# The last group of the second MLP, taken by token tile across both second-layer granules

## The chip, the cores and the metric

The kernel runs on one core of a Trainium2 chip. The metric is the device time of one execution in microseconds (us). PE is TensorE (matmuls), DVE is VectorE, ACT is ScalarE, POOL is GpSimd, SP is SyncE, which issues most transfers. SBUF is the on-chip memory, PSUM holds the eight banks that matmuls accumulate into.

## What is computed

The reference is a small network on 256 tokens of width 1024. First a block with a convolution and Fourier mixer, cross attention and a mixture of 32 experts, then two layers of attention and MLP. The change concerns only the very last step, the MLP of the second of these layers and the layer norm behind it:

```
def squared_relu_mlp(h, w1, w2):            # w1: 1024 x 4096, w2: 4096 x 1024
    return jnp.square(jax.nn.relu(h @ w1)) @ w2

y = squared_relu_mlp(h, mlp_w1[layer], mlp_w2[layer])
x = layer_norm(DN_ALPHA * x + gate * y, ln_g[layer, 1], ln_b[layer, 1])
```

All inputs are fp32, and the output is the x of 256 x 1024.

## The kernel before

**Precision.** Every fp32 product of this part is made of three matmuls in a rounded type: both operands are split into a rounded part ("hi") and a remainder ("lo"), and `three` (line 1318) issues hi x hi, hi x lo and lo x hi. So a weight granule must be rounded by ACT (`split_hi`, line 561) and its remainder taken by DVE (`split_lo`, line 572) before PE has all of it; the semaphore `w_lo` counts the remainders, and PE waits for it once per granule.

**Tiling.** Weights come in granules of 2 MB into four ring slots. An MLP has 16: even ones are a 512-column slab of `w1`, odd ones the matching 512 rows of `w2`. They are worked off in four groups (`it` = 0 to 3), each of two halves (`p` = 0, 1); half p uses granule 2p of the group for the first layer and granule 2p + 1 for the second. In the last group these are, counted over the MLP, granules 12 to 15.

**First layer of a half.** Two banks (b = 0, 1), each 8 x 2 x 3 = 48 matmuls of 256 columns; the result is the transposed hidden block, two chunks of 128 hidden units for each b. For each b ACT takes the relu (line 1086) and the square of it, rounded (line 1089), into `hid[0]`; DVE squares again in full precision into `sq_h` (line 2787) and subtracts to get the remainder into `hid[1]` (line 2791), counted by `mlp_lo`. In ACT's queue the rounding of the group's granules 2 and 3 (`split_hi`, after half 0) stands behind the square for b = 1, and in DVE's queue the two `split_lo` stand behind the subtraction for b = 1. In half 1 of the last group there is nothing left to split and nothing left to load.

**Second layer of a half.** It accumulates into banks 0 to 3: bank 2t + h is token tile t (128 tokens) and column half h (512 columns). One half of a group takes 2 (b) x 2 (r) x 2 (t) x 2 (h) x 3 = 48 matmuls of 512 columns. Normally the order is b, r, then the four banks. Only in half 1 of the last group it is t, h, b, r, so that the banks are finished one after another; each of the first three increments `ln_y0`, the last one `used`.

**The end.** The layer norm (`layer_norm`, line 2695, DVE) waits for each bank in turn. For each it multiplies with the gate (line 2706), adds the scaled x (line 2707) and takes statistics (line 2708); after both halves of a tile come the aggregate (line 2710), a root on ACT (line 1040), a reciprocal and a product (lines 2713, 2714). Tile 0 is then normalized by ACT (line 1047) and scaled and shifted by POOL (lines 838, 840); tile 1 is finished by DVE itself in two halves (lines 2723, 2724). SP stores tile 0 in one transfer (line 770) and tile 1 in two (line 773). Every engine works its instructions off in the order written; a wait holds up all that stands behind it in that engine's queue.

**Memory.** `hid` lies at 0 to 2047 of the area `arena`, `relu_h` at 2048, `sq_h` at 3072. The words from 4096 to 5119 are not used in the second MLP.

Of the kernel before, what the change touches and what calls it, by code (L numbers as in the profile page):

```python
# [19 lines left out]
F32 = mybir.dt.float32  # L20
# [7 lines left out]
P = 128  # L28
S = 256
TB = S // P  # L30
# [9 lines left out]
HW = 512  # L40
# [198 lines left out]
def build_program(nc, A, tab_d, dft_d, out_d):  # L239
    ctx = ExitStack()  # L240
    with ctx:
# [76 lines left out]
        def arn(a, w):  # L318
            return arena[:, a:a + w]

        def arn_r(a, w):
            return arena_r[:, a:a + w]
# [68 lines left out]
        lng = arn(5264, D)  # L391
        lnb = arn(6288, D)
        hid = [arn_r(a, 1024).rearrange("p (k s) -> p k s", k=4) for a in (0, 1024)]
        relu_h, sq_h = (arn(a, 1024).rearrange("p (k s) -> p k s", k=4) for a in (2048, 3072))

        def late_part(u):
# [447 lines left out]
        def _(act):  # L844
# [230 lines left out]
            def mlp_group(l, it, last, ahead=None, first=False):  # L1075

                n = f"mlp{l}"
                for p in range(2):
                    for b in range(2):
                        c = 2 * p + b + 1  # L1080
                        h = B[b if first and p == 0 else 4 + b]
                        if b == 0:
                            act.wait_ge(*upto(n, "mlp_h", it * 2 + (p + 1)))
                        else:
                            act.wait_ge(used, it * R2 + done(n, 2 * p)[1])
                        act.activation(relu_h[:, 2 * b:2 * b + 2, :], h[:].rearrange("p (k s) -> p k s", k=2),
                                       ACT.Relu, bias=zero).then_inc(sem("mlp_relu"), 1)
                        act.wait_ge(*upto(n, "mlp_relu", it * 4 + c))
                        act.activation(hid[0][:, 2 * b:2 * b + 2, :], relu_h[:, 2 * b:2 * b + 2, :], ACT.Square,
                                       bias=zero).then_inc(sem("mlp_sq"), 1)  # L1090
                    if l == 0 and last and p == 0:
                        act.wait_ge(sem("late_comb"), 12)
                        act.activation(vec[:, 0, :], B[6][:, 0:P], ACT.Copy).then_inc(sem("late_part"), 1)
                    if not (last and p == 1):
                        split_hi(act, n, 2 * p + 2, it)
                        split_hi(act, n, 2 * p + 3, it)
                    if p == 0 and ahead is not None:
                        split_hi(act, *ahead)
                    if l == 0 and last and p == 0:
                        act.wait_ge(sem("late_comb"), 13)  # L1100
                        act.activation(mod[:, 3, :], B[6][:, 256:280], ACT.Copy).then_inc(sem("late_read"), 1)
                    elif l == 0 and last:
                        gate_rows(1)
# [174 lines left out]
        def _(pe):  # L1278
# [676 lines left out]
            def mlp_group(l, it, last, first=False):  # L1955

                n = f"mlp{l}"
                for p in range(2):
                    g = at[0] + 2 * p
                    pe.wait_ge(sem("w_lo"), it * R2 + split_no(g))  # L1960
                    w = chunks(pair(g), KC)
                    if first and p == 0:
                        first_hidden(l, w)
                    for b in range(0 if first and p == 0 else 2):
                        for k in range(KC):
                            if b == 0:
                                x_chunk(2 * l + 1, max(k, 1))
                            for r in range(2):
                                f = 2 * b + r
                                mm = three(B[4 + b][:, r * S:(r + 1) * S], cut3(w, k, f * P, (f + 1) * P),  # L1970
                                           cut3((XT_r, XTL[2 * l + 1]), k, 0, S), k == 0 and r == 0, k == KC - 1)
                        mm.then_inc(sem("mlp_h") if b == 0 else used, 1)
                    if l == 0 and p == 0 and it:
                        unit_sums(it - 1)
                    if l == 0 and p == 1 and last:
                        pe.wait_ge(sem("late_read"), 3)
                        gate_rows(1)
                    g = g + 1
                    halved = l == 0 and first and p == 0
                    if halved:  # L1980
                        pe.wait_ge(sem("lo_part"), 3)
                    else:
                        pe.wait_ge(sem("w_lo"), it * R2 + split_no(g))
                    w = chunks(pair(g), 4)
                    if last and p == 1:
                        for t in range(TB):
                            for h in range(2):
                                for b in range(2):
                                    pe.wait_ge(*upto(n, "mlp_lo", it * 4 + (2 * p + b + 1)))
                                    for r in range(2):  # L1990
                                        mm = three(B[2 * t + h][:], cut3(hid, 2 * b + r, t * P, (t + 1) * P),
                                                   cut3(w, 2 * b + r, h * HW, (h + 1) * HW), False, False)
                                mm.then_inc(sem("ln_y0") if t + h < 2 else used, 1)
                        continue
                    for b in range(2):
                        pe.wait_ge(*upto(n, "mlp_lo", it * 4 + (2 * p + b + 1)))
                        if halved and b:
                            pe.wait_ge(sem("w_lo"), split_no(g))
                        for r in range(2):
                            begin = first and p + b + r == 0  # L2000
                            for t, h in ((0, 0), (1, 0), (1, 1), (0, 1)):
                                if begin and (t, h) == (0, 1):
                                    pe.wait_ge(*upto(n, "mlp_relu", 2))
                                mm = three(B[2 * t + h][:], cut3(hid, 2 * b + r, t * P, (t + 1) * P),
                                           cut3(w, 2 * b + r, h * HW, (h + 1) * HW), begin, False)
                    mm.then_inc(used, 1)
                    if l == 0 and last:
                        pe.wait_ge(sem("late_part"), 13)
                        pe.matmul(B[6][:, 256:280], vec[:, 0, :], ident.rearrange("p (c n) -> p n c", n=32)[:, 0:6, :],
                                  start=True, stop=True).then_inc(sem("late_comb"), 1)  # L2010
# [231 lines left out]
        def _(dve):  # L2242
# [536 lines left out]
            def mlp_group(l, it, last, ahead=None, first=False):  # L2779

                n = f"mlp{l}"
                for p in range(2):
                    for b in range(2):
                        c = 2 * p + b + 1
                        dve.wait_ge(*upto(n, "mlp_relu", it * 4 + c))
                        hb = slice(2 * b, 2 * b + 2)
                        dve.tensor_tensor(sq_h[:, hb, :], relu_h[:, hb, :], relu_h[:, hb, :],
                                          ALU.mult).then_inc(sem("mlp_tt"), 1)
                        dve.wait_ge(*upto(n, "mlp_tt", it * 4 + c))
                        dve.wait_ge(*upto(n, "mlp_sq", it * 4 + c))  # L2790
                        dve.tensor_tensor(hid[1][:, hb, :], sq_h[:, hb, :], hid[0][:, hb, :].bitcast(F32),  # L2791
                                          ALU.subtract).then_inc(sem("mlp_lo"), 1)
                        if first and c == 1:
                            first_out_lo(dve, 1)
                    by_unit = l == 0 and not last
                    if by_unit:
                        unit_rows(2 * it + p, 0, 3)
                    if not (last and p == 1):
                        split_lo(dve, n, 2 * p + 2, it)
                        if by_unit:  # L2800
                            unit_rows(2 * it + p, 3, 5)
                        split_lo(dve, n, 2 * p + 3, it)
                        if by_unit:
                            unit_rows(2 * it + p, 5, 8)
                    if p == 0 and ahead is not None:
                        split_lo(dve, *ahead)
                    if l == 0 and last and p == 0:
                        affine_ready(1)
                        affine("ln0", range(TB))
# [189 lines left out]
```

## Time and profile before

| | us |
|---|---|
| median of 3 runs | 1796.16 |
| lowest of them | 1792.27 |
| highest of them | 1941.92 |
| the profiled execution | 1793.1 |
| its span (first to last instruction) | 1791.3 |

Times in rows are microseconds from the start of the span. A line number is that of the kernel's code; L1321 is the helper `three`, so all split matmuls share it and are told apart by time and by the number of columns. Matmuls overlap: the duration in a row is that of one matmul from start to end, and successive ones start closer together than that.

### The profile page before, as it was taken

The page shows a single profiled execution, that of the slowest core. Times are in us where ns is not written, and L with a number is a line of the kernel's source. Part 1 is how long each engine was busy: PE and PEld are TensorE (multiplying, and loading weights), DVE is VectorE, ACT ScalarE, POOL GpSimd, SP SyncE. Part 2 cuts the span into 40 slices and gives each one's busy share as a digit, 9 for nine tenths or more (in the row PEclk, how much of TensorE's full clock was granted, in tenths as well). Part 3 has the DMA queues.
Part 4 walks back from the last instruction along what each step waited for, and adds up shares of the span by engine and source line. Part 5 has one row for each costly group of instructions (what it writes and reads, how often), then busy time and mean ns, then how long its engine had stood idle before and what let it go on. Part 6 is the DMA issues. An engine that isn't in the chain of part 4 may idle for free.

```text
span 1791.3 us, 24226 instructions
## 1 busy us (share of the span) xinstructions
PE 1724.1 (96%) x9828; PEld 1083.8 (61%) x9828; DVE 777.9 (43%) x1327; ACT 524.1 (29%) x694; POOL 33.8 (2%) x40
## 2 busy tenths in 40 slices
PE   8999999999999999999999999999999999899997
PEld 7878754443443434343434343375799988689986
DVE  4454442221221212121212121289887779676555
ACT  5353421111111111111101010247544455644442
POOL 0002000000000000000000000000000010000001
PEclk9999999999999999999999999998999999999999
DMA  9757999999999999999999999975387754335550
GB/s 347 285 200 289 371 396 429 428 427 427 428 429 428 429 428 428 429 428 429 428 428 429 428 429 428 421 283 201 118 286 269 278 205 177 124 119 188 187 210 24
DMA packets 97287, 587.54 MB, mean 328 GB/s; under 512 B 7822, under 2 KB 8036, under 8 KB 71620
## 3 DMA queue, kind: packets, MB, share of 16 engines
q1 hardware_dynamic: 95744, 582.28, 80.5%
q10 hardware_dynamic: 1476, 4.30, 0.7%
q8 instruction: 50, 0.82, 0.2%
q14 instruction: 17, 0.14, 0.0%
HBM read 585.51 MB, written 1.05 MB: 327 GB/s over the span
## 4 chain that ended last, share of the span: by engine, by line
PE 73%; DMA 20%; DVE 3%; ACT 3%; issue 1%; SPq 0%; DVEq 0%; ACTq 0%
PE bank L1321 32%; DMA ring<-in_w_gate_up 19%; PE bank L1635 15%; PE bank L1654 9%; PE bank L1581 4%; PE bank L1903 3%; PE bank L1665 1%; PE bank L1949 1%; PE bank L1627 1%; PE bank L1406 1%; ACT arena L1003 1%; PE bank L1647 1%; ACT sb_XN L1122 1%; DMA ring<-in_w_k 1%; PE bank L2160 0%
## 5 line engine op out<-in xcount | busy, mean ns | idle before, releaser
L1635 PE MATMUL bank<-ring,arena 128*64 128x512 f32 x2048 | 462.6, 597 | 29.0 <-DMA ring<-in_w_gate_up 28.8
L1635 PEld LDWEIGHTS bank<-ring,arena 128*64 128x64 f32 x2048 | 137.5, 136 | 320.2 <-issue 255.3
L1654 PE MATMUL bank<-ring,arena 128*64 128x512 f32 x1024 | 226.8, 595 | 3.3
L1321 PE MATMUL bank<-w_hi,arena_r 128*128 128x512 f32 x672 | 217.2, 392 | 0.9 <-DVE arena_r L2791 0.9
L572 DVE TENSOR_TENSOR w_lo<-ring,w_hi 128x4096 fp32r<-128x4096 f32 (+2 forms) x43 | 188.0, 4373 | 27.9 <-ACT w_hi L561 26.3
L2498 DVE TENSOR_SCALAR arena<-bank 128x512 f32<-128x512 f32 x32 | 22.1, 692 | 367.6 <-PE bank L1635 367.6
L1001 ACT ACTIVATE arena<-arena,sb_tab 128x512 f32<-128x512 f32 x32 | 23.1, 722 | 508.8 <-DVE arena L2498 508.8
L561 ACT ACTIVATE w_hi<-ring 128x4096 fp32r<-128x4096 f32 (+2 forms) x43 | 152.4, 3586 | 20.4 <-DMA ring<-in_c_w_in 12.4
L1654 PEld LDWEIGHTS bank<-ring,arena 128*64 128x64 f32 x1024 | 71.7, 137 | 137.8 <-issue 132.3
L1321 PEld LDWEIGHTS bank<-w_hi,arena_r 128*128 128x128 f32 x672 | 126.2, 188 | 29.3 <-issue 1.9
L1581 PEld LDWEIGHTS bank<-arena,sb_XN 128*128 128x128 f32 x1056 | 123.2, 192 | 26.9 <-issue 26.9
L1581 PE MATMUL bank<-arena,sb_XN 128*128 128x64 f32 x1056 | 128.4, 275 | 0.0
L1321 PE MATMUL bank<-XT_r,w_hi 128*128 128x256 f32 x448 | 127.2, 284 | 0.0
L1321 PE MATMUL bank<-arena_r,w_hi 128*128 128x256 f32 x448 | 126.8, 283 | 0.0
L1321 PE MATMUL bank<-XT_r,w_lo 128*128 128x256 f32 x448 | 126.8, 283 | 0.0
L1321 PE MATMUL bank<-w_lo,arena_r 128*128 128x512 f32 x304 | 118.5, 390 | 0.0
L2519 DVE SCALAR_TENSOR_TENSOR arena_r<-bank,sb_att,arena_r 128x512 fp32r<-128x512 f32 x32 | 24.0, 750 | 217.3 <-ACT arena_r L1006 217.3
L1006 ACT ACTIVATE arena_r<-bank,sb_att 128x512 fp32r<-128x512 f32 x32 | 22.0, 688 | 231.0 <-PE bank L1654 231.0
L545 DVE TENSOR_TENSOR half_lo<-ring,half_hi 128x2048 fp32r<-128x2048 f32 x26 | 59.5, 2290 | 67.8 <-ACT half_hi L535 67.8
L1321 PEld LDWEIGHTS bank<-XT_r,w_hi 128*128 128x128 f32 x448 | 86.0, 192 | 0.7 <-issue 0.2
L1321 PEld LDWEIGHTS bank<-arena_r,w_hi 128*128 128x128 f32 x448 | 86.0, 192 | 0.7 <-issue 0.2
L1321 PEld LDWEIGHTS bank<-XT_r,w_lo 128*128 128x128 f32 x448 | 86.0, 192 | 0.0
(427 smaller groups left out, 2187.9 us busy)
## 6 DMA issues: line engine op xcount, KB each, us to landing
ring<-in_w_gate_up SPq DMA_DIRECT2D x128, 2048.0 KB, 32.0
ring<-in_w_down SPq DMA_DIRECT2D x64, 2048.0 KB, 35.3
ring<-in_mlp_w SPq DMA_DIRECT2D x32, 2048.0 KB, 8.7
ring<-in_ada_w SPq DMA_DIRECT2D x15, 2048.0 KB, 13.3
arena<-in_ada_w SPq DMA_DIRECT2D x48, 256.0 KB, 5.5
ring<-in_c_w_in SPq DMA_DIRECT2D x6, 2048.0 KB, 8.2
ring<-in_w_in SPq DMA_DIRECT2D x4, 2048.0 KB, 8.3
ring<-in_w_v SPq DMA_DIRECT2D x2, 2048.0 KB, 24.2
```

Of the source, the lines that this page charges most:

```text
L545: eng.tensor_tensor(lo[:], half_raw(name, h)[1], hi[:].bitcast(F32), ALU.subtract).then_inc(sem("w_lo"), 1)
L561: ins = eng.activation(dst, raw, ACT.Copy) if on_act else eng.tensor_copy(dst, raw)
L572: eng.tensor_tensor(lo[:, 0:w], slot(slot_of(granule_no(name, i)), w), hi[:, 0:w].bitcast(F32), ALU.subtract).then_inc(sem("w_lo"), 1)
L1001: act.activation(sig, gcl, ACT.Sigmoid, bias=zero, scale=1.702).then_inc(sem("e_sig"), 1)
L1006: act.activation(y_hi, B[2][:], ACT.Copy, scale=slot_gate).then_inc(sem("e_y"), 1)
L1321: mm = pe.matmul(out, st[a], mv[b], start=start and a + b == 0, stop=stop and a == 1, skip_group_check=True)
L1581: mm = pe.matmul(B[3][:, k * CAP:(k + 1) * CAP], XN[:, t, k * P:(k + 1) * P], sel_tok[:, t, :], start=(t == 0), stop=(t == 1))
L1635: mm = pe.matmul(B[m][CAP * h:CAP * h + CAP, :], xe[:, 2 * j + kl, :], w[:, kl, m * D + h * HW:m * D + (h + 1) * HW], start=False, stop=(j ...
L1654: mm = pe.matmul(B[2][CAP * h:CAP * h + CAP, :], hT[:, c, CAP * j:CAP * j + CAP], w[:, c, h * HW:(h + 1) * HW], start=(j == 0 and c == 0), ...
L1903: mm = pe.matmul(b, x[:, k, t * P:(t + 1) * P], parts[wa][:, kl, width * c:width * c + width], start=k + xa + wa == 0, stop=False, skip_gr ...
L2498: dve.tensor_scalar(gcl, B[0][:], 7.0, None, ALU.min).then_inc(sem("e_clamp"), 1)
L2519: dve.scalar_tensor_tensor(y_lo, B[2][:], slot_gate, y_hi.bitcast(F32), ALU.mult, ALU.subtract).then_inc(sem("e_ylo"), 1)
```

## The change

In the last group of the second MLP (`l == 1`, `it == 3`):

- half 0 of the second layer issues only the 24 matmuls of token tile 0 (both column halves) and then counts its granule as used; its weight views are kept as `w0`;
- half 1 of the second layer issues, for tile 0, the 24 matmuls of its own granule (bank 0, then bank 1), and for tile 1, bank by bank, the 12 of half 0's granule (hidden block `hid`, weights `w0`) and then the 12 of its own;
- so that half 0's hidden block lives until then, half 1's goes into `hid_last`: its rounded part to 4096, its remainder to 3072, in place of `sq_h`.

The number of matmuls, activations and vector instructions stays the same, and so do their shapes.

```
+        hid_last = [arn_r(a, 1024).rearrange("p (k s) -> p k s", k=4) for a in (4096, 3072)]
...
-                        act.activation(hid[0][:, 2 * b:2 * b + 2, :], relu_h[:, 2 * b:2 * b + 2, :], ACT.Square,
+                        to = hid_last[0] if l == 1 and last and p == 1 else hid[0]
+                        act.activation(to[:, 2 * b:2 * b + 2, :], relu_h[:, 2 * b:2 * b + 2, :], ACT.Square,
                                        bias=zero).then_inc(sem("mlp_sq"), 1)
...
+                    if last and l == 1:
+                        if p == 0:
+                            w0 = w
+                            for b in range(2):
+                                pe.wait_ge(*upto(n, "mlp_lo", it * 4 + (b + 1)))
+                                for r in range(2):
+                                    for h in range(2):
+                                        mm = three(B[h][:], cut3(hid, 2 * b + r, 0, P),
+                                                   cut3(w0, 2 * b + r, h * HW, (h + 1) * HW), False, False)
+                            mm.then_inc(used, 1)
+                            continue
+                        for t in range(TB):
+                            for h in range(2):
+                                for x, v in ((hid, w0), (hid_last, w))[0 if t else 1:]:
+                                    for b in range(2):
+                                        if x is hid_last:
+                                            pe.wait_ge(*upto(n, "mlp_lo", it * 4 + (3 + b)))
+                                        for r in range(2):
+                                            mm = three(B[2 * t + h][:], cut3(x, 2 * b + r, t * P, (t + 1) * P),
+                                                       cut3(v, 2 * b + r, h * HW, (h + 1) * HW), False, False)
+                                mm.then_inc(sem("ln_y0") if t + h < 2 else used, 1)
+                        continue
...
-                        dve.tensor_tensor(hid[1][:, hb, :], sq_h[:, hb, :], hid[0][:, hb, :].bitcast(F32),
+                        to = hid_last if l == 1 and last and p == 1 else hid
+                        dve.tensor_tensor(to[1][:, hb, :], sq_h[:, hb, :], to[0][:, hb, :].bitcast(F32),
                                           ALU.subtract).then_inc(sem("mlp_lo"), 1)
```

## Rows read from the trace of the kernel before

**Rows 1.** The page: span, and busy time with share of each engine.

```profile
span 1791.3 us, 24226 instructions
PE 1724.1 (96%) x9828; PEld 1083.8 (61%) x9828; DVE 777.9 (43%) x1327; ACT 524.1 (29%) x694; POOL 33.8 (2%) x40
```

**Rows 2.** Chain that ended last, from 1640 us: start, duration, engine, output, line, count.

```profile
1735.38 33.95 PE bank L1321 x240
...
1771.64 9.83 PE bank L1321 x42
...
1781.50 0.70 DVE sb_XN L2706
...
1787.77 0.75 DVE sb_X L2724
```

**Rows 3.** Timeline of PE: start, duration, then instruction; in brackets idle before it.

```profile
1746.73 0.40 PE L1321 MATMUL bank<-w_hi,arena_r 128*128 128x512 f32 x1
...
1757.64 0.28 PE L1321 MATMUL bank<-XT_r,w_hi 128*128 128x256 f32 x1
...
1769.15 0.40 PE L1321 MATMUL bank<-w_hi,arena_r 128*128 128x512 f32 x1
...
1771.64 0.50 PE L1321 MATMUL bank<-w_hi,arena_r 128*128 128x512 f32 x1 [0.95 <-DVE arena_r L2791]
...
1781.07 0.39 PE L1321 MATMUL bank<-w_hi,arena_r 128*128 128x512 f32 x1
```

**Rows 4.** Timelines of ACT and DVE around the last two splits.

```profile
1747.65 0.73 ACT L1089 ACTIVATE arena_r<-arena,sb_tab 128x512 fp32r<-128x512 f32 x1
1748.28 3.61 ACT L561 ACTIVATE w_hi<-ring 128x4096 fp32r<-128x4096 f32 x1
...
1748.48 0.69 DVE L2791 TENSOR_TENSOR arena_r<-arena,arena_r 128x512 fp32r<-128x512 f32 x1
1751.93 4.42 DVE L572 TENSOR_TENSOR w_lo<-ring,w_hi 128x4096 fp32r<-128x4096 f32 x1 [2.75 <-ACT w_hi L561]
...
1770.90 0.69 DVE L2791 TENSOR_TENSOR arena_r<-arena,arena_r 128x512 fp32r<-128x512 f32 x1
```

**Rows 5.** Windows: length, busy time by engine, granted clock, DMA share, GB/s.

```profile
1220.00:1225.00 5.00, 4.08 (x25) 1.02 (x28) 4.55 (x17) 4.18 (x15) 0.00 (x0) 0.66 0.18 73
1231.00:1238.00 7.00, 7.00 (x30) 3.74 (x30) 6.69 (x31) 5.93 (x10) 0.00 (x0) 0.51 0.37 138
...
1771.00:1772.00 1.00, 0.36 (x2) 0.32 (x3) 0.59 (x1) 0.00 (x0) 0.00 (x0) 1.00 0.00 0
...
1781.50:1784.00 2.50, 0.00 (x0) 0.00 (x0) 2.43 (x3) 0.00 (x0) 2.42 (x2) 0.99 0.00 0
1784.00:1791.30 7.30, 0.00 (x0) 0.00 (x0) 4.02 (x8) 0.30 (x1) 1.74 (x1) 0.50 0.37 144
```

**Rows 6.** Timeline of PE just before the granted clock fell at 1221 us.

```profile
1218.23 0.49 PE L2125 MATMUL bank<-arena 64*128 64x128 f32 x2 [0.66 <-ACT arena L1200]
...
1220.93 5.23 PE L1821 MATMUL bank<-ring,sb_cs 128*32 128x512 f32 x32 [0.92 <-ACT arena L1200]
```

**Rows 7.** Timelines of DVE and POOL around PE's last matmul.

```profile
1779.85 0.69 DVE L2707 SCALAR_TENSOR_TENSOR sb_X<-sb_X,sb_XN 128x512 f32<-128x512 f32 x1
...
1782.22 1.32 DVE L2707 SCALAR_TENSOR_TENSOR sb_X<-sb_X,sb_XN 128x512 f32<-128x512 f32 x1
1783.58 0.69 DVE L2708 BATCH_NORM_STATS2 sb_rt<-sb_X 128x6 f32<-128x512 f32 x1
...
1785.21 1.08 DVE L2723 SCALAR_TENSOR_TENSOR sb_X<-sb_X,sb_att,arena 128x512 f32<-128x512 f32 x1
...
1786.99 0.74 DVE L2723 SCALAR_TENSOR_TENSOR sb_X<-sb_X,sb_att,arena 128x512 f32<-128x512 f32 x1
...
1780.64 2.35 POOL L838 TENSOR_TENSOR sb_X<-sb_X,arena 128x1024 f32<-128x1024 f32 x1 [245.21 <-ACT sb_X L1047]
1783.08 2.67 POOL L840 TENSOR_TENSOR sb_X<-sb_X,arena 128x1024 f32<-128x1024 f32 x1
```

## The prediction

> **What bounds the kernel now.** I read the page's head first: the span is 1791.3 us and TensorE (PE) is busy for 1724.1 us of it, 96% [rows 1]. A share that large says that nearly everything that PE does later is paid in full, but it is an average, so the next view was the chain of the work that ended last, cut to the last 150 us. The reader is to see there that the chain stays on PE until PE's last matmul, with one interruption, and then runs over VectorE (DVE) to the end [rows 2]. So the change is costed on two stretches: PE from the last group of the second MLP on, and the 10 us behind its last matmul.
>
> The timeline of PE gives the calendar of that group. Its first activation granule (L1 below: 96 matmuls of 256 columns) ends at 1746.73, where the 48 matmuls of 512 columns of the second layer's first granule begin (granule 13, "L2a"). L1 of the second half (granule 14) begins at 1757.64, the last second-layer granule (15, "L2b") at 1769.15, and the last matmul ends at 1781.07 + 0.39 = 1781.46 [rows 3]. L2a takes 1757.64 - 1746.73 = 10.91 us, so one 512-column matmul is worth 10.91/48 = 0.227 us; the "0.39" of a row is its latency, not its price. L1 takes 1769.15 - 1757.64 = 11.51 us.
>
> The timelines of ScalarE (ACT) and DVE show what L1 of the second half needs. ACT rounds granule 14 (line 561, 3.61 us) only after the square for the second half of the first hidden block (line 1089), and DVE takes the remainder (line 572) right behind it: 1751.93 + 4.42 = 1756.35 [rows 4]. PE asks for it at 1757.64, so today it has 1.29 us to spare.
>
> **The change, part by part.** *L2a loses half its matmuls.* PE now issues only the 24 for token tile 0. That takes 24 x 0.227 = 5.46 us, to 1746.73 + 5.46 = 1752.19. Within it, the second hidden pair is needed after 12 matmuls, at 1749.46, and its remainder is finished at 1748.48 + 0.69 = 1749.17 [rows 4]: no stall, by 0.3 us.
>
> *L1 of the second half meets a new wait.* Its weights are complete at 1756.35, and nothing in the diff moves that: ACT's order is the same, and ACT and DVE start these splits as soon as the preceding step is done: 1747.65 + 0.73 against 1748.28, and 1748.28 + 3.61 against 1751.93 [rows 4]. PE stands from 1752.19 to about 1756.40 (the handover from DVE to PE at the 0.95 us stall took 1771.64 - 1770.90 - 0.69 = 0.05 us [rows 3, 4]). Queued behind the waiting instruction is all the rest of PE's program; DVE, ACT and the output wait for that. So of 5.46 us moved away, only 1757.64 - 1756.40 = 1.24 us comes back as an earlier start, and 4.2 us becomes idle time.
>
> *The 24 matmuls come back at the end.* For token tile 1 PE runs 12 old plus 12 new matmuls per column half: + 5.46 us between the end of L1 and the end of PE. From L1's end to PE's end it was 1781.46 - 1769.15 = 12.31 us, with the 0.95 us stall before the second hidden pair, and that stall stays: the tile 0 work starts with the same 6 matmuls as before and then waits for the same DVE step [rows 3]. The deferred matmuls, which need nothing new, could have covered it, but they are queued behind tile 0.
>
> Net at PE's end: + 5.46 - 1.24 = + 4.22 us.
>
> *The clock.* At the end of the kernel the granted clock was 0.99 over the 2.5 us behind the last matmul and 0.50 (1.2 instead of 2.4 GHz) after that [rows 5]. Around 1220 us it fell when PE had idled only 0.92 us just before the matmul at 1220.93, after other gaps, and it averaged 0.66 over 5 us, that is (1 - 0.66) x 2 x 5 = 3.4 us low; around 1231 it averaged 0.51 over 7 us, 6.9 us low, although PE was working [rows 5, 6]. So I expect the 4.2 us stop to cost a low stretch under L1. Work in it runs at half rate, so the loss is half of it: 1.7 us for 3.4 us, 3.4 us for 6.9 us, and 0 if the clock holds. I take 1.7, since dense matmuls follow the stop as they followed the one at 1220.93.
>
> On this the Trainium skill (TensorE: Matmul & The Clock Gate, section Why this matters for your kernels) speaks against this change: it says to leave no idle gaps between bursts of matmuls, because the clock then falls back to half. The trace agrees: idle time stands before each fall I looked at [rows 5, 6]. By that rule the sum is the one with a fall, without it the sum is 1.7 us less.
>
> *The layer norm behind PE.* Tile 0 is done, as before, 24 matmuls after L1's end, but behind it PE now works on tile 1 for 48 matmuls, 10.9 us, instead of for 24, 5.46 us. GpSimd (POOL) works on tile 0 from 1780.64 to 1783.08 + 2.67 = 1785.75, of which 4.29 us lie behind PE's end; now that work ends 5.46 us earlier against PE's end, 1.2 us before it. Under it today one DVE step of line 2707 takes 1.32 us where its twin took 0.69, and the first of line 2723 takes 1.08 where the second, after POOL is done, takes 0.74 [rows 7]. Both are on the path behind PE. Gain: 0.63 + 0.34 = 0.97 us. The rest of the path behind PE is unchanged: before, 1788.52 (the end of the chain, 1787.77 + 0.75) - 1781.46 = 7.06 us of DVE and ACT, now 6.1. The last store's 2.8 us (1788.52 to 1791.3) also stays; the tile 0 store moves ahead of it, for which I take nothing.
>
> The GpSimd page of the Trainium skill (GPSIMD Engine Reference, section Key points) says that it shares its SBUF interfaces with VectorE when that has two SBUF inputs. The trace agrees: the stretched steps have two SBUF inputs, and line 2708 with one keeps its 0.69 us while POOL works [rows 7]. Were this not the cause, the 0.97 us would stay and the sum be that much longer.
>
> *The activations in a place of their own.* ACT's square and DVE's subtraction write elsewhere, same shapes, same counts; 0. No transfer and no entry in SP's or POOL's queue moves, and the semaphore counts that others wait for keep their order. The early count for granule 13 frees nothing: this is the last group, so no transfer and no split waits for that slot.
>
> **Sum**, against the profiled execution's span of 1791.3: + 4.22 (PE) + 1.7 (clock) - 0.97 (layer norm) = + 4.95, a span of 1796.3; with the 1.8 us around it (1793.1 against 1791.3), 1798.1. The median of the runs shown, 1796.16, lies 3.1 us above the profiled execution and the lowest, 1792.27, lies 0.8 below, so an execution after may read 1797.3 to 1801.1. I forecast 1799.
>
> **Rivals.** (a) *The clock holds*: + 3.2 us, 1794.5 of span. For it: the stall of 0.95 us in this group left the clock at 1.00 [rows 5]. Against it: rows 5 and 6. (b) *The clock stays low for two such stretches*, 6.9 us: + 6.7 us, 1798.0 of span. For it: it did so at 1231. Against: the matmuls there were small and sparse, here they are dense. (c) *No new stall, and a gain*: if granule 14's remainder were ready by 1752.19, PE would lose nothing (+ 5.46 - 5.46) and the layer norm's 0.97 us would be won: 1790.3 of span. What decides is when one DVE step ends, now 1756.35: the kernel breaks even with today if it ends 3.25 us earlier, at 1753.1. Against it: ACT has no free time before it, since line 561 follows line 1089 without a gap. (d) *The clock stays low to the end of PE*: the 11.5 us of L1 and 72 matmuls of 0.227 us, together 27.9 us, would take twice that; with the + 3.2 us of (a), + 31 us, 1.7%. Nothing in the trace kept the clock low under dense matmuls. (e) *The change does nothing measurable*: that holds in all these cases but (d) for a plain comparison, since 5 us are 0.3%.
>
> **How the numbers follow.** Chances: the forecast with one low stretch 0.62, (a) 0.2, (b) 0.12, (c) 0.04, (d) 0.02. (a) to (c) with the spread of executions (-0.8 to +3.1 about the profiled one) reach from 1791.3 to 1802.9; leaving out (c), with a margin of 2 us for another session, the range is 1794 to 1805. Faster by over 2% (what a measurement of this kernel can tell from no change) would need 36 us less, for which no case has a mechanism: 0.01. Slower by over 2%: (d) with something on top, 0.01. Within 2%: 0.98.
>
> **What would show it.** PE idle for about 4 us before the first L1 matmul of granule 14, waiting for DVE line 572, near 1752 us; a granted clock under 1 right after it, for about 3.4 us; the 0.95 us stall before the second hidden pair unchanged; 66 matmuls in a row behind it, 15 us; POOL's two steps finished before PE's last matmul, and all four DVE steps of lines 2707 and 2723 for tile 1 near 0.7 us. PE's end near 1787.4 on the time axis of before. If the wait is missing or under 1 us, the first step is wrong; if the clock stays at 1.00, the second.

## The result and the profile after

The changed kernel takes 1800.70 us (median of 9 runs, 1797.56 to 1866.6) against 1795.31 us of the kernel before (median of 9, the three runs shown ahead of the prediction and six later ones). The ratio is 1.0026 with a 95% interval of 1.0017 to 1.0035: 5 us slower, clear of noise, and far inside the 2% that a plain comparison of this kernel can tell. The highest value of each kernel is a disturbed run, which the ratio leaves out. The forecast was 1799 us, 1794 to 1805.

The profiled execution after has a span of 1795.7 us against 1791.3. Part of every such difference is made elsewhere: the kernels below, nearly the same up to there, reach the last group of the second MLP at times that differ by up to 4.7 us (1734.81 to 1739.56), and two executions of the changed kernel at 1735.03 and 1737.28. So all profiles are compared from the start of that group, which is the end of the gate rows (the matmuls of line 1754), to the end of the span: 1791.3 - 1735.38 = 55.9 us before [rows 2], 1795.7 - 1735.03 = 60.7 us after. The group and what follows it got 4.8 us longer; the 0.35 us between this and the 4.4 us of the spans was won before the group and means nothing. One profile each is enough for this, because the measure repeats: 60.7 us again in the second profile of the changed kernel (experiment 8), and 55.9 us in experiments 4 and 5, where nothing should change it.

The chain of work that ended last, after (start, duration, engine, output, line, count; line numbers are those of the changed kernel, up to 24 above those of before):

```profile
1735.03 11.53 PE bank L1323 x96
...
1746.58 0.70 ACT arena L1087
...
1747.93 3.62 ACT w_hi L562
...
1751.58 4.44 DVE w_lo L573
...
1756.06 13.27 PE bank L1323 x96
...
1770.90 0.70 DVE arena_r L2816
...
1771.65 15.27 PE bank L1323 x66
...
1786.94 0.70 DVE sb_XN L2730
...
1792.25 0.75 DVE sb_X L2748
```

Before, the chain stayed on PE from 1735.38 through 240 matmuls up to the second stop [rows 2]. Now it leaves PE after the first 96, because the next thing that PE waits for is granule 14, and runs over ACT's rounding and DVE's remainder back to PE. The 96 matmuls behind it fill 13.27 us where 96 of the same kind fill 11.53 a few rows above. The 66 of the end fill 15.27 us, 0.231 us each, about the price of before (9.83/42 = 0.234).

The waits of PE in this stretch (engine, output, line, releaser: total, times, longest), after:

```profile
PE bank L1323 <- DVE w_lo L573: 4.0, 1, 4.0
PE bank L1323 <- DVE arena_r L2816: 0.9, 1, 0.9
```

The second is the old stop of 0.95 us [rows 3]; the first is new. The windows of after (columns as in rows 5) show the clock in the stop, behind it, and after that:

```profile
1751.80:1756.00 4.20, 0.21 (x1) 0.00 (x0) 4.20 (x1) 3.25 (x1) 0.00 (x0) 1.00 0.00 0
1756.30:1759.70 3.40, 3.40 (x18) 3.40 (x18) 3.40 (x1) 0.00 (x0) 0.00 (x0) 0.50 0.03 5
1759.70:1769.00 9.30, 9.30 (x79) 9.30 (x79) 2.22 (x3) 1.41 (x2) 0.00 (x0) 1.00 0.00 0
```

The granted clock stood at 1.00 in the stop. PE resumed at 1756.06, and from 1756.30 the clock was at its lower level (1.2 GHz), for 3.4 us, all of it under matmuls. In the timeline of PE (start, duration), two neighbours at either level:

```profile
1758.21 0.41 PE L1323 MATMUL bank<-arena_r,w_hi 128*128 128x256 f32 x1
1758.42 0.41 PE L1323 MATMUL bank<-XT_r,w_lo 128*128 128x256 f32 x1
...
1759.69 0.28 PE L1323 MATMUL bank<-XT_r,w_lo 128*128 128x256 f32 x1
1759.82 0.28 PE L1323 MATMUL bank<-XT_r,w_hi 128*128 128x256 f32 x1
```

They start 0.21 us apart at the lower level and 0.12 to 0.13 at the higher. Behind PE's end, DVE and POOL, after:

```profile
1782.23 1.36 DVE L2731 SCALAR_TENSOR_TENSOR sb_X<-sb_X,sb_XN 128x512 f32<-128x512 f32 x1
...
1787.67 0.69 DVE L2731 SCALAR_TENSOR_TENSOR sb_X<-sb_X,sb_XN 128x512 f32<-128x512 f32 x1
...
1790.02 0.74 DVE L2747 SCALAR_TENSOR_TENSOR sb_X<-sb_X,sb_att,arena 128x512 f32<-128x512 f32 x1
...
1780.65 2.39 POOL L839 TENSOR_TENSOR sb_X<-sb_X,arena 128x1024 f32<-128x1024 f32 x1 [245.57 <-ACT sb_X L1048]
1783.12 2.73 POOL L841 TENSOR_TENSOR sb_X<-sb_X,arena 128x1024 f32<-128x1024 f32 x1
```

POOL is done at 1785.85, 1.1 us before PE's last matmul ends (1786.91). The stretched DVE step is now that of tile 1's first half. It is off the path, since DVE stands idle for 2.6 us before the bank of the second half is ready; the last step of line 2731 is at 0.69 us and the first of line 2747 at 0.74, where they took 1.32 and 1.08 [rows 7]. From PE's end to DVE's end it is 6.1 us instead of 7.06.

### The profile page after: what moved, and what is told of

Read it like the earlier page. It is cut to its first block, busy times and chain, and to the rows that moved or that the text cites. A ratio compares the mean times of both kernels' runs of the same rounds, so it can differ in the third digit from the quotient of the medians.

```text
span 1795.7 us, 24226 instructions
## 1 busy us (share of the span) xinstructions
PE 1725.5 (96%) x9828; PEld 1085.6 (60%) x9828; DVE 777.8 (43%) x1327; ACT 523.7 (29%) x694; POOL 33.9 (2%) x40
## 4 chain that ended last, share of the span: by engine, by line
PE 72%; DMA 20%; DVE 4%; ACT 3%; issue 1%; SPq 0%; DVEq 0%; ACTq 0%
PE bank L1323 32%; DMA ring<-in_w_gate_up 19%; PE bank L1637 15%; PE bank L1656 9%; PE bank L1583 4%; PE bank L1905 3%; PE bank L1667 1%; PE bank L1951 1%; PE bank L1629 1%; PE bank L1408 1%; ACT arena L1004 1%; PE bank L1649 1%; ACT w_hi L562 1%; ACT sb_XN L1124 1%; DMA ring<-in_w_k 1%
```

## The experiments

The theory: the moved matmuls cost nothing by themselves. The kernel loses because PE now reaches granule 14 before it is split, stands still, and resumes at a low clock; it wins back 1 us because POOL is out of DVE's way. The rivals: the new order is slower in itself (many matmuls into one bank, two weight areas, the new place of the hidden block); the clock fell by chance, or its fall is not on the path; DVE's long steps behind PE have another cause. "Group" below is the time from the group's start to the end of the span, one profiled execution each: 55.9 us before, 60.7 after. Experiments 2, 5, 7, 8 and 9 have one run each, the profiled one.

**1. Filling the stop, first try.** After the 24 matmuls of granule 13, on top of the change:

```
+                            pe.wait_ge(*upto("ln3", "gate", 2))
+                            keep_busy(6, 9)
```

> The changed kernel, with nine extra fp32 matmuls of the identity into the unused bank 6 issued between the 24 matmuls of granule 13 and the wait for granule 14; their results are not read. They take 9 x 0.43 = 3.9 us (the four such matmuls of the gate rows took 1.72 us), a little less than the 4.05 us stop. Theory (the stop costs twice: 4.2 us of standing and a low clock behind it): PE is no longer idle there, the granted clock stays at 1.00, the first layer of the second half takes 11.5 instead of 13.1 us, and the span is 1.6 us shorter than that of the changed kernel, near 1794.1, while granule 14's remainder still comes at the same time. Rival (the clock fell for another reason, or its fall cost nothing on the path): the first layer stays at 13.1 us and the span at 1795.7.

Measured: 1801.77 us, ratio to before 1.0043 [1.0028, 1.0058]; group 62.7 us. The fill was mis-sized. Its row in the chain of this kernel, with the two around it (start, duration, engine, output, line, count, as in all chains below):

```profile
1737.44 16.99 PE bank L1323 x120
1754.43 7.73 PE bank L1314 x18
1762.15 11.53 PE bank L1323 x96
```

An fp32 matmul of the code is two on the chip, 18 for 9, so the fill took 7.7 us and delayed the first layer itself. (The 1.72 us that the expectation puts down to four matmuls of the gate rows are two in the code, which the chain counts as four.) As a test of the sum it still serves: no stop before granule 14, no low clock, 96 matmuls in 11.53 us, and the 66 behind them in 15.3 as in the changed kernel.

**2. Filling the stop, second try.** The same with `keep_busy(6, 4)`.

> The fill again, with four matmul calls in place of nine: on the chip one fp32 call had become two matmuls, 18 instead of 9, so the fill had outlasted the stop by 3.5 us. Now 8 x 0.43 = 3.4 us lie in the 4.05 us stop and end before granule 14 is complete. Theory: the first layer of the second half begins when it did in the changed kernel, counted from the start of the group, and takes 11.5 instead of 13.1 us; from the start of the group (the first matmul of its first layer) to the end of the span it is 60.7 - 1.6 = 59.1 us. Rival (the low clock costs nothing on the path): 60.7 us.

Measured (one run): group 1797.3 - 1738.02 = 59.3 us. The chain:

```profile
1754.57 4.43 DVE w_lo L573
...
1759.04 11.79 PE bank L1323 x96
...
1773.16 15.28 PE bank L1323 x66
```

The granted clock was 1.00 until PE's last matmul, and PE's first layer took 11.79 instead of 13.27 us, although it began at the same place, right behind DVE's step and 21.0 us after the group's start in both. That is the price of the clock alone: 1.48 us. Expected were 11.5 us and a group of 59.1; what is left over is no matter of the clock. The fill ended 0.6 us before granule 14 was complete, and the timeline of PE shows what a resumption costs at full clock:

```profile
1759.04 0.38 PE L1323 MATMUL bank<-XT_r,w_hi 128*128 128x256 f32 x1 [0.60 <-DVE w_lo L573]
1759.27 0.28 PE L1323 MATMUL bank<-arena_r,w_hi 128*128 128x256 f32 x1
1759.39 0.28 PE L1323 MATMUL bank<-XT_r,w_lo 128*128 128x256 f32 x1
```

The second matmul starts 0.23 us behind the first, the third 0.12 us behind the second: 0.11 us lost. The other 0.15 of the 0.26 us between 11.79 and 11.53 are a matter of counting: in an unbroken run the piece of the chain begins where the matmul before it ends, with the next one already under way, and behind a stop it begins with a matmul's start. Experiment 6 has the same 0.26 us, behind a stop of 1.3 us at full clock.

**3. The wait removed.** On top of the change, ACT rounds granule 14 before its gate rows, and DVE takes the remainder before the group's first hidden block. ACT's half of the edit and the head of DVE's:

```
+            split_hi(act, "mlp1", 2, 3)
             gate_rows(3)
...
+                early = l == 1 and last
...
+                        if not early:
                             split_hi(act, n, 2 * p + 2, it)
...
+                if early:
+                    split_lo(dve, n, 2, it)
```

> The changed kernel, with granule 14 rounded by ACT before its gate rows and its remainder taken by DVE before the first hidden block of the last group, so that it is complete near 1741 instead of 1756 us. Theory (the whole loss comes from that one wait): PE starts the first layer of the second half at about 1752.2 without a stop, the clock stays at 1.00, PE ends where it ended in the kernel before (near 1781.5), and the path behind PE stays at 6.1 us: 5.8 us less than the changed kernel, 1.0 us less than the kernel before, a span near 1790. Rival (the order by tile itself costs, by accumulating many matmuls in one bank or by reading two weight areas): PE ends later than 1781.5 although no stop is left, and the kernel stays slower than before. Second rival: the early split delays the first hidden block on ACT or DVE and the stop moves to the second layer of the first half.

Measured: 1794.38 us, ratio to before 0.9995 [0.9986, 1.0004]; group 1789.8 - 1734.85 = 54.95 us. The chain:

```profile
1734.85 28.51 PE bank L1326 x216
...
1765.67 15.27 PE bank L1326 x66
```

The chain no longer leaves PE for granule 14, and PE's only wait left is the one of 0.9 us. The group is 5.7 us shorter than after the change and 0.95 shorter than before. PE needs 1780.94 - 1734.85 = 46.09 us for its 288 matmuls, the 46.08 of the kernel before. So the whole loss hangs on that one wait, and the order by tile costs nothing in itself. In executions as a whole the 1 us left is below what 11 runs can tell.

**4. The control: the same early split in the kernel before.** The edit of experiment 3, on the old order.

> The kernel before, with the same early split of granule 14 and nothing else. It is the control for the previous one. Theory: PE had 1.29 us to spare on granule 14, so its earliness is worth nothing here: span within 0.5 us of 1791.3, PE's end at 1781.5, the path behind PE 7.1 us with the POOL overlap. Rival (the early split itself speeds something up or disturbs the first hidden block): a span that moves by 1 us or more.

Measured: 1794.18 us, 0.9999 [0.9989, 1.0008]; group 1790.9 - 1735.03 = 55.9 us, and in the chain the stretched DVE step:

```profile
1781.87 1.35 DVE sb_X L2710
```

Without the new order the early split is worth nothing: granule 14 was in time already.

**5. The place alone.** The second half's hidden block in its own place, but all 48 matmuls of granule 13 in the first half. This and experiments 6, 7, 10 and 11 write the order as two lists. In the first half each hidden pair b has its list of banks (t, h); in the second each bank (t, h) has its parts (late, b, t, h), six matmuls each, late = 0 for hidden block and weights of the first half:

```
+                            for b, banks in [(0, [(0, 0), (0, 1), (1, 0), (1, 1)]), (1, [(0, 0), (0, 1), (1, 0), (1, 1)])]:
...
+                        for t, h, parts in [(0, 0, [(1, 0, 0, 0), (1, 1, 0, 0)]), (0, 1, [(1, 0, 0, 1), (1, 1, 0, 1)]), (1, 0, [(1, 0, 1, 0), (1, 1, 1, 0)]), (1, 1, [(1, 0, 1, 1), (1, 1, 1, 1)])]:
+                            for late, b, t_, h_ in parts:
+                                if late:
+                                    pe.wait_ge(*upto(n, "mlp_lo", it * 4 + (3 + b)))
+                                mm = six(hid_last if late else hid, w if late else w0, b, t_, h_)
```

> The other part of the change alone: the second half's hidden block goes into the place of its own, but all 48 matmuls of granule 13 are issued in the first half as before (order: hidden pair, bank, chunk), so nothing is put off. Theory: the place costs nothing, no stop before granule 14: 55.9 us from the start of the group to the end of the span, as before. Rival (writing over sq_h in place, or reading the hidden block from another place, costs time on DVE or PE): line 2791's counterpart over 0.69 us or the last 48 matmuls over 12.3 us.

Measured (one run): group 1793.3 - 1737.37 = 55.9 us, the last 42 matmuls in 9.83 us as before [rows 2], DVE's step behind them at 1.34 us. The place costs nothing.

**6. Half of the matmuls put off.** 12 instead of 24 (tile 1, column half 1); against the lists of experiment 5:

```
+                            for b, banks in [(0, [(0, 0), (0, 1), (1, 0)]), (1, [(0, 0), (0, 1), (1, 0)])]:
...
+                        for t, h, parts in [(0, 0, [(1, 0, 0, 0), (1, 1, 0, 0)]), (0, 1, [(1, 0, 0, 1), (1, 1, 0, 1)]), (1, 0, [(1, 0, 1, 0), (1, 1, 1, 0)]), (1, 1, [(0, 0, 1, 1), (0, 1, 1, 1), (1, 0, 1, 1), (1, 1, 1, 1)])]:
```

> The changed kernel, but only the 12 matmuls of tile 1, column half 1 are put off; 36 are issued in the first half. Theory: they end at 1754.9, the stop before granule 14 is 1.5 us, the start of the first layer is the same (1756.4), PE has 12 x 0.227 = 2.7 us more behind it: PE's end is 1.5 us later than before if the clock holds over so short a stop, 3.2 if it falls. POOL ends 1.6 us behind PE, so the step of line 2723 is back at 0.74 us and that of line 2707 is still stretched: 0.3 to 0.6 us gained. Sum +1.0 us against before (near 1792.3) with the clock held, +2.7 with a fall. Rival (each deferred matmul costs more than its 0.227 us): more than half of the 24-matmul kernel's +4.4 us.

Measured: 1796.15 us, 1.0009 [0.9999, 1.0018]; group 1796.5 - 1739.56 = 56.9 us, + 1.0 as the theory had it with the clock held. The wait was 1.3 us and the windows (columns as in rows 5) show the clock at 1.00 behind it:

```profile
1757.00:1760.60 3.60, 2.27 (x11) 1.53 (x10) 3.53 (x1) 2.58 (x1) 0.00 (x0) 1.00 0.00 0
1760.60:1764.00 3.40, 3.40 (x28) 3.40 (x29) 3.36 (x1) 0.00 (x0) 0.00 (x0) 1.00 0.00 0
```

**7. 18 of them put off.** All but the 6 of tile 1, column half 0, first hidden pair; against the lists of experiment 5:

```
+                            for b, banks in [(0, [(0, 0), (0, 1), (1, 0)]), (1, [(0, 0), (0, 1)])]:
...
+                        for t, h, parts in [(0, 0, [(1, 0, 0, 0), (1, 1, 0, 0)]), (0, 1, [(1, 0, 0, 1), (1, 1, 0, 1)]), (1, 0, [(0, 1, 1, 0), (1, 0, 1, 0), (1, 1, 1, 0)]), (1, 1, [(0, 0, 1, 1), (0, 1, 1, 1), (1, 0, 1, 1), (1, 1, 1, 1)])]:
```

> 18 of the 24 matmuls put off (all but tile 1, column half 0, first hidden pair). Between the 12 of e4, where the stop was 1.3 us and the clock held, and the 24, where it was 4.05 us and fell. The stop is now 1756.4 - 1753.55 = 2.8 us. PE's end is 18 x 0.227 - 1.24 = 2.85 us later, POOL ends 0.2 us behind PE and touches no step on the path, so - 0.97: 57.8 us from the start of the group to the end of the span if the clock holds over such a stop, up to 1.7 us more (59.5) if it falls.

Measured (one run): group 1798.3 - 1738.88 = 59.4 us. PE waited 2.7 us for granule 14, and the clock fell:

```profile
1757.20:1759.90 2.70, 0.02 (x1) 0.00 (x0) 2.65 (x1) 1.70 (x1) 0.00 (x0) 1.00 0.00 0
1760.30:1763.60 3.30, 3.30 (x17) 3.30 (x17) 3.30 (x1) 0.00 (x0) 0.00 (x0) 0.50 0.02 5
```

The first layer took 13.29 us, as in the changed kernel. So the clock's 1.5 us is paid behind a stop of 2.7 or 4.05 us and was not paid behind one of 1.3, nor behind the 0.6 of experiment 2. One profile of a length (two of 4.05) doesn't say where between them it begins, nor that the clock always falls.

**8. The changed kernel once more.** No edit.

> The changed kernel once more, unchanged, for the clock alone: how much of the low stretch lies under matmuls depends on when in the stop the clock falls. Theory: stop of 4.05 us again, low clock again, first layer between 11.8 us (the low stretch mostly inside the stop) and 13.3 us (all of it under work); 59.1 to 60.9 us from the start of the group to the end of the span. Rival (the fall in the first profile was chance): granted clock 1.00 throughout, 59.1 us.

Measured (one run): group 1798.0 - 1737.28 = 60.7 us, the wait 4.1 us, the first layer 13.28 us. The clock fell a little later against the resumption (its 1 us window from 1758 reads 0.85, where PE resumed at 1758.31) and the price was the same.

**9. POOL out of the way.** The kernel before without POOL's product and sum on tile 0, a memset of one column in their place. Tile 0 of the output lacks the last gain and shift.

```
-            pool.tensor_tensor(X[:, 0, :], X[:, 0, :], lng, ALU.mult).then_inc(sem("mod_g"), 1)
-            pool.wait_ge(sem("mod_g"), 5)
-            pool.tensor_tensor(X[:, 0, :], X[:, 0, :], lnb, ALU.add).then_inc(sem("y0_out"), 1)
+            pool.memset(stat[:, 126:127], 0.0).then_inc(sem("y0_out"), 1)
```

> The kernel before without POOL's two steps on tile 0 (the product with the gain of the last layer norm and the sum with its shift), a small memset in their place; tile 0 of the output lacks them. It measures the disputed part behind PE by itself. Theory (POOL's two steps slow the DVE steps that read two operands from SBUF): line 2707's last step falls from 1.32 to 0.69 us and the first of line 2723 from 1.08 to 0.74, the path behind PE from 7.06 to 6.09 us. Rival (the stretched steps come from something else, such as ACT's or DVE's own order): both stay long.

Measured (one run): group 1789.7 - 1734.81 = 54.9 us, 1.0 less than before. Its timeline behind PE:

```profile
1781.65 0.69 DVE L2705 SCALAR_TENSOR_TENSOR sb_X<-sb_X,sb_XN 128x512 f32<-128x512 f32 x1
...
1784.01 0.74 DVE L2721 SCALAR_TENSOR_TENSOR sb_X<-sb_X,sb_att,arena 128x512 f32<-128x512 f32 x1
```

Both steps fell to their short value (0.69 and 0.74 us). The stretch comes from POOL.

**10. Six matmuls into the old stop.** Only 6 are put off (tile 1, column half 1, second hidden pair), and they are issued between the first 6 matmuls of tile 0 and the wait for the second hidden pair. No early split.

```
+                            for b, banks in [(0, [(0, 0), (0, 1), (1, 0), (1, 1)]), (1, [(0, 0), (0, 1), (1, 0)])]:
...
+                        for t, h, parts in [(0, 0, [(1, 0, 0, 0), (0, 1, 1, 1), (1, 1, 0, 0)]), (0, 1, [(1, 0, 0, 1), (1, 1, 0, 1)]), (1, 0, [(1, 0, 1, 0), (1, 1, 1, 0)]), (1, 1, [(1, 0, 1, 1), (1, 1, 1, 1)])]:
```

> The changed kernel, but only 6 matmuls (tile 1, column half 1, second hidden pair) are put off, and they are issued in the second stop, between the first 6 matmuls of tile 0 and the wait for the second hidden pair of the second half. Theory: the 42 issued in the first half reach 1756.3, where granule 14 is just complete (1756.4), so the stop is 0.1 us; the first layer starts 1.2 us earlier than before, and the 0.95 us stop behind it is filled. PE's end comes 0.9 us earlier than in the kernel before (1.2 from the earlier start, with the 0.95 us stop closed but 1.37 us of matmuls in it); the path behind PE stays at 7.1 us, since tile 0 is done no earlier against PE's end. 55.0 us from the start of the group to the end of the span, against 55.9 before. Rival (the stops are not what counts but the amount of work behind the last layer's start): as before, 55.9 us or more.

Measured: 1793.91 us, 0.9992 [0.9983, 1.0001]; group 1792.1 - 1737.22 = 54.9 us. The chain of this group is one piece, without a wait of PE:

```profile
1737.22 45.09 PE bank L1323 x288
```

All 288 matmuls in 45.09 us, where they spanned 1781.46 - 1735.38 = 46.08 before [rows 2, 3]. PE still loses about 0.2 us at granule 14, too short for the profile to call it a wait. In its timeline the next matmul starts 0.36 us behind the last of 512 columns (0.227 us in a row), and the one behind that after 0.22 us (0.12):

```profile
1757.89 0.39 PE L1323 MATMUL bank<-w_hi,arena_r 128*128 128x512 f32 x1
1758.25 0.38 PE L1323 MATMUL bank<-XT_r,w_hi 128*128 128x256 f32 x1
1758.47 0.28 PE L1323 MATMUL bank<-arena_r,w_hi 128*128 128x256 f32 x1
```

The stretched DVE step stays at 1.32 us, since tile 0 is no earlier against PE's end. In executions as a whole the 1 us isn't clear of noise.

**11. Both: early split as in experiment 3, 24 put off, 6 of these in the old stop.**

```
+                            for b, banks in [(0, [(0, 0), (0, 1)]), (1, [(0, 0), (0, 1)])]:
...
+                        for t, h, parts in [(0, 0, [(1, 0, 0, 0), (0, 0, 1, 0), (1, 1, 0, 0)]), (0, 1, [(1, 0, 0, 1), (1, 1, 0, 1)]), (1, 0, [(0, 1, 1, 0), (1, 0, 1, 0), (1, 1, 1, 0)]), (1, 1, [(0, 0, 1, 1), (0, 1, 1, 1), (1, 0, 1, 1), (1, 1, 1, 1)])]:
```

> The changed kernel with the early split of granule 14, and of the 24 matmuls put off, 6 (tile 1, column half 0, first hidden pair) are issued in the second stop. Theory: no stop is left in the group. PE's end comes 0.95 us earlier than in the kernel with the early split alone, POOL's work on tile 0 ends just as PE does, so the path behind PE stays at 6.1 us: 54.0 us from the start of the group to the end of the span (55.9 before, 54.95 with the early split alone). Rival: tile 0 is done 0.4 us later and POOL still overlaps line 2707's last step, which gives back up to 0.6 us.

Measured: 1792.20 us (median of 11 runs), ratio to before 0.9980 [0.9971, 0.9989]; group 1789.5 - 1735.86 = 53.6 us. It beats the kernel before by 2.3 us in the group and by 0.2% as a whole, and the changed kernel by 7.1 us in the group. Chain and last DVE step:

```profile
1735.86 44.85 PE bank L1326 x288
...
1781.46 0.70 DVE sb_X L2734
```

The expected 54.0 was 0.4 too much. PE's 288 matmuls take 1.23 us less than before, not 0.95: the 0.95 us are counted from the end of the matmul before the stop, 0.16 us behind the start that the next one could have had, and the slow first start behind the stop (0.1 us) goes too.

## Why the prediction was right

The place of the loss, its mechanism and the sum came out; the group grew by 4.8 us where the sum said 4.95. Of this, PE's end moved by 5.80 us (5.92 in the sum), the path behind it by - 0.97 (the same), and the last store behind that took 0.1 us less (2.7 for 2.8), which the sum didn't have.

*No stall within the first half:* right. No wait of PE stands between the 24 matmuls of granule 13.

*A new wait for granule 14, of 4.2 us:* right, 4.05 us of idle time from the end of the last matmul, and 4.2 from the moment at which the next one could have started, which is what the sum counted. Experiment 3 shows that nothing else is lost, and experiment 4 that the split's time mattered to nobody before. Summed by what PE does, the loss is plainer than in the prediction's bookkeeping of 5.46 away and 5.46 back: same matmuls, plus a stop of 4.2, plus 0.11 of slow resumption (experiment 2), plus 1.48 of low clock, 5.8 us. It was measured as 1786.91 - 1735.03 = 51.88 against 46.08.

*The clock, 1.7 us (0 to 3.4):* right in kind, slightly too large. The low stretch was 3.4 us, as taken from the row at 1220 us, but work in it doesn't run at half rate: 256-column matmuls start 0.21 us apart against 0.12, a factor of 1.8 and not 2; what holds the faster ones at 0.12 no run shows. Hence 1.48, by experiment 2. The 0.11 us of slow resumption, which the sum lacked, makes up for half of the difference.

*The second stop stays:* right, 0.94 us. That the put-off matmuls could have covered it was said, and experiments 10 and 11 show it.

*The layer norm, - 0.97 us:* right (7.06 to 6.09 us), and POOL is the cause, as named (experiment 9). One sign of it was wrong: of the four steps of lines 2707 and 2723 for tile 1, that were all to be near 0.7 us, the first took 1.36. POOL's work ends before PE does, but it still meets the step for tile 1's first half, and only because nothing waits for that step does it cost nothing.

*Rivals.* (a), the clock holds, fell: it was low in both profiles of this kernel. (b), two low stretches, fell: there was one in each. (c), no stall and a gain, did not happen but is the very kernel of experiment 3: its estimate, 55.9 - 0.97 us for the group, stands against 54.95. (d) fell: the clock was back at 1.00 from 1759.70. (e) held as it was put: the 5 us stay within 2%, and only many runs together, or the comparison by group, make them plain.

*The level of the median:* the profiled execution was foreseen at 1798.1 us and read 1797.56; the median, 1800.7, lies 3.1 us above it, the same distance as in the three runs before. The forecast of 1799 was set between the sum on top of the profiled execution (1798.1) and the sum on top of the median (1801.1), and the second came out. With the early part differing by up to 4.7 us between executions, a forecast to 2 us of a median was luck as much as working; the group's 4.8 us was not.

## What to carry to other kernels

Work that is put off is not free because it is done later anyway: it was the cover for a preparation that other engines make meanwhile. Before moving matmuls away from a place, look at how much the next operand's readiness has to spare there (here 1.3 us against 5.5 moved), and either prepare it earlier or put off only as much as there is slack; put-off work belongs in front of an existing wait, not behind it. A stop can cost more than itself: behind those of 2.7 and 4.05 us the clock fell and took another 1.5 us, behind those of 0.6 and 1.3 us it did not. And compare profiles from the last common point ahead of the edit, since the span carries the noise of everything before it.

## What the runs showed of the hardware

The stretched DVE steps are not slow, they wait. In all profiles in which POOL works on tile 0 (every one but that of experiment 9) such a step, with two operands in SBUF, ends 0.54 or 0.55 us after the POOL instruction during which it began, whenever it began: 16 cases, of 1.08 to 2.72 us. In the kernel of experiment 11 one began 0.2 us after POOL and took almost four times its 0.69 us:

```profile
1775.81 2.39 POOL L839 TENSOR_TENSOR sb_X<-sb_X,arena 128x1024 f32<-128x1024 f32 x1 [240.85 <-ACT sb_X L1048]
...
1776.03 2.72 DVE L2734 SCALAR_TENSOR_TENSOR sb_X<-sb_X,sb_XN 128x512 f32<-128x512 f32 x1
```

POOL ends at 1778.20, DVE at 1778.75; in the kernel before the same two ends are 1780.64 + 2.35 = 1782.99 and 1782.22 + 1.32 = 1783.54 [rows 7]. The step that reads one operand from PSUM (line 2730 of after) keeps 0.69 us under POOL. POOL waits in its turn: its second instruction took 2.67 to 2.73 us wherever such a DVE step was still running when it began, and 2.36 in experiment 6, the only profile where none was:

```profile
1786.18 2.36 POOL L841 TENSOR_TENSOR sb_X<-sb_X,arena 128x1024 f32<-128x1024 f32 x1
```

The Trainium skill (SBUF — State Buffer, section SBUF: two separate sides) says this of a DVE instruction with two SBUF inputs and a GpSimd instruction that reads SBUF: the one that starts first has the pair of ports that they share for its whole instruction, and the other blocks. The trace agrees, except that a step that waited ends 0.54 us behind POOL, sooner than its full 0.69 or 0.74; what part of it ran before is not shown. By that rule the 0.97 us is a matter of which POOL instruction a step meets, and how late, not of a rate; the prediction had it as a slowdown, at the same price here.

An fp32 matmul of 512 columns in the code is two matmuls of 0.43 us on the chip (7.73 us for 18 in experiment 1), which matters to anyone who sizes a filler.
